# A dead strip of 32 bytes between the loaded weights and their two rounded parts

## The reference: a two-layer trunk in float32

```python
x  = x  + 0.5*mod[2] * swiglu(modulate(rmsnorm(x),  mod[0], mod[1]), ffn1_wi, ffn1_wo)   # the same for xc
h  = modulate(rmsnorm(x), mod[3], mod[4])
zq, zk, zv, zb, zc, zu, zga, zgb = split(h @ w_in)
o  = attention(rope(q), rope(k), v, context keys and values, sink)
y  = zb * short_conv(zc * zu)
x  = x + mod[5] * ((sigmoid(zga) * (o @ w_oa) + sigmoid(zgb) * (y @ w_ob)) @ w_out)
x  = x  + 0.5*mod[8] * swiglu(modulate(rmsnorm(x), mod[6], mod[7]), ffn2_wi, ffn2_wo)
```

## The kernel before

| tiles | place | modulo 64 | modulo 128 | after the change, modulo 64 | modulo 128 |
|---|---|---|---|---|---|
| `hH`, `hL` (column 0) | 32960, 49344 | 0 | 64 | 0 | 64 |
| `hH`, `hL` (column 112) | 33408, 49792 | 0 | 0 | 0 | 0 |
| `nearH`, `nearL` | 32896, 49280 | 0 | 0 | 0 | 0 |
| `raw` | 65728 | 0 | 64 | 0 | 64 |
| `wH`, `wL` | 82112, 98496 | 0 | 64 | 32 | 96 |
| `T`, `cst` | 114880, 123072 | 0 | 64 | 32 | 96 |
| `GH`, `GL` (column 0) | 138944, 184000 | 0 | 64 | 32 | 96 |
| `GH`, `GL` (column 112) | 139392, 184448 | 0 | 0 | 32 | 32 |
| `QS`, `YH`, `YL` (column 0) | 138944, 159424, 167616 | 0 | 64 | 32 | 96 |

## Time and profile before

### The profile page before, as it was taken

One profiled execution on the slowest core, in us unless ns is written; L12 is line 12 of the kernel. 1 busy time (PEld: TensorE's weight loads), 2 busy tenths in 40 slices (PEclk: granted clock), 3 DMA queues, 4 the chain that ended last, 5 costly groups with the idle time before them and its releaser, 6 DMA issues.

```text
span 1809.7 us, 26047 instructions
## 1 busy us (share of the span) xinstructions
PE 1791.7 (99%) x9993; PEld 1541.8 (85%) x9993; DVE 1155.0 (64%) x1503; ACT 704.8 (39%) x1111; POOL 99.8 (6%) x174
## 2 busy tenths in 40 slices
PE   9999999999999999999999999999999999999998
PEld 6888888898888889888888898888888889999998
DVE  5888737656564266888738668888322587676554
ACT  3433332146344324433332144333321475556553
POOL 0110001010000001000001010100000100000000
PEclk9999999999999999999999999999999999999999
DMA  9766427423222223666427436664232245546653
GB/s 336 239 196 195 143 93 253 130 71 107 79 71 82 86 85 132 192 195 194 143 90 256 131 119 191 191 195 149 94 105 93 71 145 143 149 148 208 193 192 115
DMA packets 187892, 271.48 MB, mean 150 GB/s; under 512 B 25388, under 2 KB 154908, under 8 KB 187804
## 3 DMA queue, kind: packets, MB, share of 16 engines
q1 hardware_dynamic: 168912, 202.74, 36.6%
q0 software_dynamic: 18432, 67.12, 12.1%
q10 hardware_dynamic: 460, 0.39, 0.1%
HBM read 269.16 MB, written 1.05 MB: 149 GB/s over the span
## 4 chain that ended last, share of the span: by engine, by line
PE 92%; DVE 4%; ACT 1%; SPq 1%; issue 1%; DMA 1%; DVEq 0%; ACTq 0%
PE ps L594 23%; PE ps L595 23%; PE ps L596 23%; PE scored L594 3%; PE scored L596 2%; PE scored L595 2%; PE turned L594 2%; PE turned L595 2%; PE turned L596 2%; PE ps L655 2%; PE ps L669 2%; PE ps L659 2%; DVE wL L1391 1%; PE turned L968 1%; SPq L437 1%; PE scored L937 1%
## 5 line engine op out<-in xcount | busy, mean ns | idle before, releaser
L1391 DVE TENSOR_TENSOR wL<-raw,wH 128x1024 fp32r<-128x1024 f32 x362 | 441.2, 1223 | 453.1 <-ACT wH L1086 452.4
L1086 ACT ACTIVATE wH<-raw 128x1024 fp32r<-128x1024 f32 x364 | 383.1, 1057 | 660.1 <-PE ps L596 647.4
L594 PE MATMUL ps<-hH,wH 128*128 128x512 f32 (+1 forms) x1592 | 580.1, 364 | 0.6 <-ACT T L1187 0.6
L595 PE MATMUL ps<-hL,wH 128*128 128x512 f32 (+1 forms) x1592 | 578.1, 363 | 0.0
L596 PE MATMUL ps<-hH,wL 128*128 128x512 f32 (+1 forms) x1592 | 578.0, 363 | 0.0
L594 PEld LDWEIGHTS ps<-hH,wH 128*128 128x128 f32 x1592 | 298.9, 188 | 51.8 <-issue 3.6
L596 PEld LDWEIGHTS ps<-hH,wL 128*128 128x128 f32 x1592 | 298.9, 188 | 48.3
L595 PEld LDWEIGHTS ps<-hL,wH 128*128 128x128 f32 x1592 | 298.9, 188 | 47.0
L594 PE MATMUL ps<-GH,wH 128*128 (+2 forms) x376 | 131.5, 350 | 0.0
L596 PE MATMUL ps<-GH,wL 128*128 (+2 forms) x376 | 131.2, 349 | 0.0
L595 PE MATMUL ps<-GL,wH 128*128 (+2 forms) x376 | 131.2, 349 | 0.0
(11 more groups left out here) (247 smaller groups left out, 2523.7 us busy)
## 6 DMA issues: line engine op xcount, KB each, us to landing
raw<-in_ffn_wi SPq DMA_DIRECT2D x176, 512.0 KB, 3.7
raw<-in_ffn_wo SPq DMA_DIRECT2D x88, 512.0 KB, 3.5
raw<-in_w_in SPq DMA_DIRECT2D x60, 512.0 KB, 3.9
adaC<-in_w_ada POOLq DMA_DIRECT2D x48, 512.0 KB, 4.6
adaW<-in_w_ada POOLq DMA_DIRECT2D x32, 512.0 KB, 4.6
adaA<-in_w_ada POOLq DMA_DIRECT2D x24, 512.0 KB, 4.4
adaB<-in_w_ada POOLq DMA_DIRECT2D x24, 512.0 KB, 4.7
raw<-in_w_out SPq DMA_DIRECT2D x16, 512.0 KB, 3.4
```

Of the source, the lines that this page charges most:

```text
L594: mm(dst, wa, ra, start=start, stop=False, **kw)
L595: mm(dst, wa, rb, start=False, stop=False, **kw)
L1086: av(wH[:, s, :], raw[:, s, :], ACT.Copy).then_inc(hi_done, 1)
L1391: tt(wL[:, s, :], raw[:, s, :], wH[:, s, :].bitcast(F32), ALU.subtract).then_inc(lo_done, 1)
```

## The change

A tile of 32 bytes that nobody uses is allocated behind `raw` and in front of `wH`. `wH`, `wL` and all tiles behind them move up by 32 bytes. `X`, `hH`, `hL`, `nearH`, `nearL`, `adaW` and `raw` stay where they are. No instruction is added, removed or moved on any engine, and no wait is changed; the addresses of operands are all that differs.

```diff
@@ -81,6 +81,9 @@
 LEAD = 16
 
 
+HALF_LINE = 8
+
+
 def span(t):
 
     at = SHORT_AT if t == SEQ else 0
@@ -170,6 +173,7 @@
         adaW = sb("adaW", [P, 4, D])
         sb("low_rows", [P, 4, D])
         raw = sb("raw", [P, RING, PIECE])
+        sb("parts_lead", [P, HALF_LINE])
         wH = sb("wH", [P, RING, PIECE], F32R)
         wL = sb("wL", [P, RING, PIECE], F32R)
         T = sb("T", [P, 4, TOK])
```

## The result

The changed kernel took 1843.72 us in the median of 4 runs (1842.74 to 1844.82), the kernel before, run beside it, 1814.64 (1812.4 to 1818.37). The ratio is 1.0164, with a 95% interval of 1.0149 to 1.018. The forecast was 1815 us and no difference that can be measured, with a range up to 1842: it was wrong. The profiled execution took 1844.68 us, its span is 1842.5, so 32.8 us more than the span of before.

What follows compares the result with a forecast made beforehand. TensorE was taken as the bound: number of matmuls times the distance between their starts. Three parts summed to 0 to 4.4 us; 2 us was chosen, so 1812.98 + 2 gave 1815 us, with a range from 1806 to 1842.

Steps and rivals of the forecast that it cites:

- part (1): Stationary operand of every product starts mid-line, touching nine lines; costs 0 to 2.8 us on 256-column matmuls, nothing on 512.
- the rival: 512-column matmuls in steady state slowed by loads, 7 ns each on about 5400: 38 us, 1851 us; chance 0.14.
- the pattern: Narrow matmuls' pace depends partly on where moving rows start modulo 128 bytes; up to 6.5 ns for a pair.
- Nine lines in place of eight: An operand's 512 bytes starting mid-line touch one 64-byte line more, 0.8 ns at most per load.
- parts 1 and 2: Mid-line stationary operands, 0 to 2.8 us, and mid-line moving operands in GH/GL, QS, YH/YL, 0 to 0.7 us.
- Part (3): Mid-line operands of ScalarE, VectorE, GpSimd and DMAs: nothing on the engines, 0 to 0.9 us for DMAs in the opening.
- the wide matmuls too: The second rival: about 5400 matmuls with 512 columns lose 7 ns each, 38 us, to 1851 us; chance 0.14.
- The first: Rival: layer 1's fast 256-column matmuls fall to the slow pace, losing up to 14.4 us, 1827 us; chance 0.22.
- The gain: Rival: slow 256-column matmuls in last pieces, openings and projections become fast, 6.4 us and 1 us more, 1806 us; chance 0.20.
- the four cases: Forecast with nothing at all 0.44, narrow stretches' loss 0.22, wide ones' loss 0.14, gain 0.20.
- 16-byte lines: Reading in which 32 bytes are two SBUF lines, no operand touches more lines, the sum is 0 and the time 1813.

Runs made afterwards that it cites:

- e5: Changed kernel with a strip of 128 bytes in place of 32 in front of wH: 1840.05 us, ratio 1.0137 to the kernel before.
- e6: Changed kernel with a strip of 256 bytes in place of 32 in front of wH: 1815.66 us, ratio 1.0 to the kernel before.
- e1: Changed kernel with hH, hL, nearH, nearL, adaW and raw also moved half a line (32 bytes): 1815.18 us, ratio 0.9994 to the kernel before.
- e4: Changed kernel with a strip of 64 bytes in place of 32 in front of wH: 1841.74 us, ratio 1.0154 to the kernel before.
- m2: Products alone, not the trunk: one stationary tile, 32 moving tiles in 16-byte steps; 226.7 to 234.7 ns for 512 columns, 113.3 to 120.0 for 256.
- e7: Kernel before with layer 1's narrow rows at column 28 for 112, nearH and nearL 176 bytes further on, 256-byte strip before wH: 1811.81 us, ratio 0.9989.
- e9: Kernel before with layer 1's narrow rows alone starting at column 28 in place of 112: 1812.26 us, ratio 0.9984.
- m1: Products alone, not the trunk: pairs of stationary and moving tiles at several places modulo 128, 48 times each; blocks from 226.7 to 234.4 ns.
- e2: Kernel before with only wH and wL moved 32 bytes; 96 bytes behind wL keep later tiles' places modulo 128: 1855.46 us, ratio 1.0225.

## Why the prediction was wrong

**The step that failed** is in part (1): "With 512 columns a load has half of the matmul's time to spare, and nothing comes of it." I took the load for the one that gives way. It is the matmul that becomes longer, 233.3 ns for 226.7 with wide rows, for as long as the two streams keep their difference. On 3939 wide matmuls this was 24.9 us of the 34.5. Rows 8 had shown it, 240 ns behind a break, and I used them for the rival only, since the steady state got out of it. The reason for that was the difference of 0, not the spare time.

**The second error was the pattern.** From three narrow cases I concluded on places of the moving rows modulo 128. What counts is the difference of both, modulo 256. The 0, 64 and 0 of my list were 192, 0 and 192 in it. The dependence was seen rightly, and its size for the narrow rows too (6.5 ns at most); with a pattern read from three points there was no telling where 32 bytes more would lead. e5 and e6 were needed for it.

**Nine lines in place of eight** (parts 1 and 2, 0 to 2.8 and 0 to 0.7 us) don't show: e1 has every operand of a product in mid-line, its wide distance is 226.9 ns as before, and its time 0.9994 of before.

**Part (3)** was right: `YH <- cY` 624 ns, `hH <- GB`, now with `GB` in mid-line, 630, roundings 1223 and 1060, the packets of the first 30 us at 327 GB/s after 329.

**The rivals.** The second, "the wide matmuls too", is what happened, at 0.14. Its price, 38 us for all wide ones, was too high by those on `GH`, `QS` and `YH`, which moved along and lost nothing. The size for one, 7 ns, was good (6.4). The first happened beside it: narrow rows lost 9.6 us with openings and not 14.4, 4.6 ns each on `hH` and not 6.5. The matmuls on `GH` in layer 1's last product lost 2 us at an unchanged difference, 192. That they took the second of its two paces is seen (117.9 ns for 113.4), and in e5 as well (117.4). What chose it isn't: in e4 they stood at 113.4 behind `hH` at 118.8, in e1 at 113.9 behind 117.2. The gain was not to be had in layer 0's last pieces beyond 1.7 ns each. The range failed because the two slow rivals were priced one by one, and came together: 1813 and 24.9 us would have stayed under 1842, and with the 9.6 of the narrow rows the time came out 1.7 us above it. The chances don't add up either: by the four cases slower gets 0.36 at most and the same 0.48, and I wrote 0.38 and 0.46.

The Trainium skill's rule in "TensorE: Matmul & The Clock Gate", section "Step-by-step: what each phase is for", that loading the next weights takes no read bandwidth from the running matmul, is not borne out here: m2 has nothing on the chip but loads and matmuls while it measures, and 226.7 and 233.3 ns for the same work at different addresses. That the moving stream loses read bandwidth is the likeliest reading, but no row shows the reads themselves. What I had drawn from the Trainium skill's 16-byte lines ("SBUF — State Buffer", section "Specifications (TRN2)"), that 32 bytes would leave the time at 1813 us, fell with the change itself; no run shows how long a line is.

## What to carry to other kernels

Where each matmul loads its own stationary operand in fp32r, the difference between the places of the moving and the stationary rows, modulo 256 bytes, is a parameter. Keep it at 0 for 512 columns: every block and kernel here at 0 settled at 226.7 to 226.9 ns. For 256 try 112, and measure it: it was fast in e7, e9 and m2, and at 120.0 ns in m1. Other types, and weights that stay for several matmuls, were not tried. A dead strip or a tile of odd size between the two operands cost 1.4 to 1.6% of the whole time here without any instruction changing, 2.25% in e2, and its opposite, moving both, cost nothing. Read the distance of starts from the timeline, not durations or busy shares; and when runs of one kernel fall into groups, compare distances before looking for noise.

## What I had not expected of the hardware

- Wide products took 226.7 ns at a difference of 0, and 228.9 to 234.7 ns at nearly all others, with a period of 256 bytes (m2, e4 to e6); m1 had 226.7 at 16 too, and once at 112.
- Narrow ones took 120.0 ns at 0, where wide ones are fastest, and 113.3 at 112 and, on some ways in, at 192 (m2, e7 to e9); but in m1 112 had 120.0.
- One set of addresses can have two lasting paces, 113.3 and 117.8 or 226.7 and 233.3 ns (m1, m2). Runs of the kernel before spread from 1811.5 to 1819.5 us, and with the narrow rows at another difference the spread was gone (e7 to e9).
- Starting all operands 32 bytes into a line of 64 made no difference to any engine (e1: 0.9994).
- Which of the two reads is delayed by which, and why at some differences only, was not seen; a moving operand of one repeated column (218.7 ns) was faster than any with real rows (226.7 at best).
